# A two-layer transformer block in float32: one plain matmul for each weight product in place of three of split parts, a ring of wider weight units without loops, and a feed-forward in one pass

## What is computed

```python
def swiglu(h, w_in, w_out):
    g, u = jnp.split(h @ w_in, 2, axis=-1)
    return (jax.nn.silu(g) * u) @ w_out          # w_in 1024 x 5632, w_out 2816 x 1024

def adaln(cond, prm):                            # two rows of cond, mod_w 1024 x 9216
    mod = jax.nn.silu(cond) @ prm["mod_w"] + prm["mod_b"]
    return jnp.split(mod, N_MOD, axis=-1)

def half_ffn(x, m, name):
    sh, sc, g = m
    h = modulate(rms_norm(x, prm[name + "_norm"]), sh, sc)
    return x + 0.5 * g * swiglu(h, prm[name + "_w_in"], prm[name + "_w_out"])
```

## Time and profile before

| | us |
|---|---|
| median of 3 runs | 4154.09 (4153.86 to 4158.08) |
| span of the profiled execution | 4147.5 |
| PE busy | 3665.2 (88%), 21992 matmul records |
| DVE busy | 2043.7 (49%) |
| ACT busy | 1508.2 (36%) |
| POOL busy | 263.8 (6%) |
| DMA | 478.14 MB, 115 GB/s on average |

### The profile page before, as it was taken

How to read it: one execution, slowest core, us unless ns; L and a number is a source line. 1 busy time by engine, 2 the same in 40 slices (tenths; PEclk the granted TensorE clock), 3 DMA queues, 4 the chain that set the end, 5 groups by cost and what they waited for, 6 DMA issues and landing times. The chain is left out here.

```text
span 4147.5 us, 57916 instructions
## 1 busy us (share of the span) xinstructions
PE 3665.2 (88%) x21992; PEld 3092.6 (75%) x21992; DVE 2043.7 (49%) x2625; ACT 1508.2 (36%) x1826; POOL 263.8 (6%) x182
## 2 busy tenths in 40 slices
PE   6899987788999999988889898967999998769898
PEld 5688842366887678866579898846889898648898
DVE  6733347444334743331455555455455555554455
ACT  3522311233223532221244444334344544253343
POOL 0000010100001000020100102110000102200001
PEclk9999998899999999999899999978999999878999
DMA  8633330012334923342026565501646565204464
GB/s 263 206 84 104 87 77 32 21 31 82 96 88 144 300 78 100 83 105 81 1 79 180 148 182 153 158 1 36 165 136 178 161 179 170 77 0 107 135 172 133
DMA packets 807729, 478.14 MB, mean 115 GB/s; under 512 B 33413, under 2 KB 806004, under 8 KB 807428
## 3 DMA queue, kind: packets, MB, share of 16 engines
q1 hardware_dynamic: 797200, 473.13, 39.8%
q10 hardware_dynamic: 10356, 2.63, 0.4%
HBM read 474.65 MB, written 1.05 MB: 115 GB/s over the span
## 5 line engine op out<-in xcount | busy, mean ns | idle before, releaser
L469 PE MATMUL psum<-normed,weights_part 128*128 128x256 f32 (+1 forms) x11232 | 1732.9, 316 | 92.5 <-DVE normed L1025 32.6
L469 PEld LDWEIGHTS psum<-normed,weights_part 128*128 128x128 f32 x11232 | 1588.2, 192 | 231.6 <-issue 89.6
L453 DVE TENSOR_TENSOR weights_part<-weights,weights_part 128x2048 fp32r<-128x2048 f32 x460 | 1053.0, 2292 | 806.3 <-ACT weights_part L445 805.7
L445 ACT ACTIVATE weights_part<-weights 128x2048 fp32r<-128x2048 f32 x460 | 878.3, 1912 | 866.7 <-PE psum L469 360.0
L469 PE MATMUL psum<-hidden,weights_part 128*128 128x256 f32 (+1 forms) x4224 | 681.0, 323 | 10.6 <-DVE hidden L1037 10.6
L469 PEld LDWEIGHTS psum<-hidden,weights_part 128*128 128x128 f32 x4224 | 615.4, 190 | 74.3 <-DVE hidden L1037 12.7
L398 POOL TENSOR_TENSOR square<-square,rinvs 128x256 f32<-128x256 f32 (+1 forms) x52 | 82.5, 1586 | 2694.6 <-ACT rinvs L383 2691.7
L469 PE MATMUL psum<-weights_part,cond_part 128*2 128x256 f32 x1728 | 214.2, 280 | 13.8 <-DVE weights_part L453 13.8
L469 PEld LDWEIGHTS psum<-weights_part,cond_part 128*2 128x2 f32 x1728 | 138.8, 83 | 70.0 <-issue 14.5
L1035 DVE TENSOR_TENSOR rinvs<-rinvs,psum 128x256 f32<-128x256 f32 (+1 forms) x88 | 45.5, 517 | 174.1 <-ACT rinvs L947 174.1
L1047 DVE SCALAR_TENSOR_TENSOR x<-psum,gate,x 128x256 f32 (+1 forms) x112 | 49.7, 480 | 163.6 <-PE psum L469 163.5
(11 more groups left out here) (295 smaller groups left out, 3136.6 us busy)
## 6 DMA issues: line engine op xcount, KB each, us to landing
weights<-in_l_ffn_w_in SPq DMA_DIRECT2D x176, 512.0 KB, 5.0
weights<-in_ffn_w_gu SPq DMA_DIRECT2D x176, 512.0 KB, 5.0
weights<-in_l_mod_w SPq DMA_DIRECT2D x72, 1024.0 KB, 5.1
weights<-in_w_in SPq DMA_DIRECT2D x34, 1024.0 KB, 5.0
weights<-in_w_gate SPq DMA_DIRECT2D x64, 512.0 KB, 4.8
weights<-in_l_ffn_w_out SPq DMA_DIRECT2D x64, 384.0 KB, 4.1
weights<-in_ffn_w_down SPq DMA_DIRECT2D x64, 384.0 KB, 4.1
weights<-in_l_ffn_w_out SPq DMA_DIRECT2D x64, 320.0 KB, 3.4
```

Of the source, the lines that this page charges most:

```text
L445: nc.scalar.activation(k.parts[part][0][:, :], k.slots[slot][:, 0:WIDE], ACT.Copy).then_inc(high.sem, 1)
L453: nc.vector.tensor_tensor(k.parts[part][1][:, :], k.slots[slot][:, 0:WIDE], k.parts[part][0][:, :].bitcast(F32), ALU.subtract).then_inc(lo ...
L469: mm = k.nc.tensor.matmul(to, left[a], right[b], start=first and n == 0, stop=last and n == len(PASSES) - 1)
```

## The change

1. Every split product becomes one plain float32 matmul. `split_high`, `split_low`, `product_of_parts`, the part buffers and the splits of activations are gone.
2. The ring is one area of 15360 words in each partition, in which units of their own size follow each other; a unit may be loaded when the last unit that overlapped its place is done. A feed-forward up unit is now a pair of hidden chunks (2 MB, 4096 words), a down unit 256 output columns over 11 chunks (2816 words), a conditioning unit 512 columns (2 MB), a merge unit 256 columns of one branch. The loops of four are written out.
3. The feed-forward is one pass: 11 up units, then 8 down units, with all 22 hidden chunks in memory. A sum over 22 chunks stays in its bank.
4. DVE adds the squares, all but the last, which the matmul with ones now takes as a second matmul into the same bank. In the conditioning ACT copies the products out of PSUM.

```diff
-def product_of_parts(k, to, left, right, first, last):
-
-    for n, (a, b) in enumerate(PASSES):
-        mm = k.nc.tensor.matmul(to, left[a], right[b], start=first and n == 0, stop=last and n == len(PASSES) - 1)
-    return mm
...
+def place_units(k):
+    units = [u for spec in k.plan for u in spec.units]
+    head, raised = 0, [0] * LANDINGS
+    for j, u in enumerate(units):
+        if head + u.words > RING_WORDS:
+            head = 0
+        u.at = head
+        head += u.words
+        u.slot = k.ring[:, u.at:u.at + u.words]
+        shared = [i + 1 for i, v in enumerate(units[:j]) if v.at < u.at + u.words and u.at < v.at + v.words]
+        u.free_after = max([0, j - LANDINGS + 1] + shared[-1:])
...
+def load_weights(k, sp, done):
+    while k.loaded < len(k.units) and k.units[k.loaded].free_after <= done:
+        u = k.units[k.loaded]
+        if u.free_after:
+            sp.wait_ge(*k.units[u.free_after - 1].done)
+        for dst, src in u.load(u.slot):
+            sp.dma_start(dst, src).then_inc(k.weights_ready[u.landing], 16)
+        k.loaded += 1
...
+def sum_of_squares(k, bank, tokens):
+    total, buffers = square_buffers(k, tokens)
+    k.nc.tensor.matmul(bank, k.const("ones"), total, start=True, stop=False)
+    return k.nc.tensor.matmul(bank, k.const("ones"), buffers[(KD - 1) % 2], start=False, stop=True)
...
 def half_ffn(k, tokens, name, layer, gain, shift, gate):
...
         @block.tensor
         def _(pe):
-            nc.tensor.matmul(k.psum[:, 0, T], k.const("ones"), k.square[:, 0, T], start=True, stop=True)\
-                .then_inc(t["summed"].sem, 1)
...
+            sum_of_squares(k, k.psum[:, 0, T], tokens).then_inc(t["summed"].sem, 1)
+            for c in range(PAIRS):
+                W = wait_weights(k, pe, up, c).rearrange("p (t k c) -> p t k c", t=2, k=KD)
+                places = [(2 * c + half, side) for half in range(2) for side in range(2)]
+                order = [(n, side, kc) for n, side in places for kc in range(KD)]
+                if c == 0:
+                    pe.wait_ge(t["inverse_done"].sem, t["inverse_done"].base + 1)
+                    order = [(n, side, kc) for kc in range(KD) for n, side in places]
+                for n, side, kc in order:
+                    if (n, side) == (0, 0):
+                        pe.wait_ge(t["normed"].sem, t["normed"].base + kc + 1)
+                    if n >= 4 and (side, kc) == (0, 0):
+                        pe.wait_ge(t["gated"].sem, t["gated"].base + n - 3)
+                    at = (n % 2) * P
+                    mm = nc.tensor.matmul(k.psum[:, 2 * (n % 4) + side, T], W[:, side, kc, at:at + P], k.normed[:, kc, T],
+                                          start=kc == 0, stop=kc == KD - 1)
...
+            for c in range(8):
+                W = tiled(wait_weights(k, pe, down, c), KH, 256)
+                for u in range(2):
+                    chunk, half = (c // 2) * 2 + u, c % 2
+                    for kc in range(KH):
+                        n = half * KH + kc
+                        if chunk == 0:
+                            pe.wait_ge(t["gated"].sem, t["gated"].base + max(n + 1, KF - 2))
...
+                        mm = nc.tensor.matmul(k.psum[:, (chunk + 4) % 8, T], W[:, kc, u * P:(u + 1) * P], k.hidden[:, n, T],
+                                              start=n == 0, stop=n == KF - 1)
...
 def conditioning(k, l):
...
             def unit(i, c):
-                slot, weights = wait_parts(pe, i, c)
                 for kc in range(KD):
-                    mm = product_of_parts(k, k.psum[0:2, 2 * slot, 0:256], [x[:, kc, :] for x in cond_parts],
-                                          [wide_tile(w)[:, kc, :] for w in weights], kc == 0, kc == KD - 1)
+                    mm = nc.tensor.matmul(k.psum[0:2, c % 4, :], k.cond[:, kc, :], W[:, kc, :], start=kc == 0, stop=kc == KD - 1)
```

More of the change, by code:

```diff
@@ L481, in _ @@
         def _(act):
-            if splits is not None:
-                splits[0](act, 0, 0)
             act.wait_ge(mean.sem, mean.base + 1)
@@ L494, in _ @@
                                                bias=shift(c, cond), scale=gain(c, cond))
-            if parts is not None:
-                for c in range(KD):
-                    act.wait_ge(scaled.sem, scaled.base + 2 + c)
-                    k.nc.scalar.activation(parts[0][:, c, T], dst[:, c, T], ACT.Copy).then_inc(high.sem, 1)
         @block.tensor
         def _(pe):
-            k.nc.tensor.matmul(k.psum[:, 0, T], k.const("ones"), k.square[:, 0, T], start=True, stop=True)\
-                .then_inc(mean.sem, 1)
+            sum_of_squares(k, k.psum[:, 0, T], tokens).then_inc(mean.sem, 1)
         @block.vector
         def _(dve):
-            if splits is not None:
-                splits[1](dve, 0, 0)
             dve.wait_ge(root.sem, root.base + 1)
@@ L585, in add_product_of_parts @@
-    high.close(KD), low.close(KD)
+            for n in range(KD):
+                dve.wait_ge(formed.sem, formed.base + n + 1)
+                for cond, part in (halves(tokens) if gate is not None else [(0, T)]):
+                    row, product = k.x[:, n, part], k.psum[:, n, part]
+                    if gate is None:
+                        last = nc.vector.tensor_tensor(row, row, product, ALU.add)
+                    else:
+                        last = nc.vector.scalar_tensor_tensor(row, product, gate(n, cond), row, ALU.mult, ALU.add)
+                last.then_inc(added.sem, 1)
+                if n >= 2:
+                    add_square(k, dve, tokens, n - 1)
@@ new lines, in _ @@
+            if shift is not None:
+                for c in range(KD):
+                    act.wait_ge(t["scaled"].sem, t["scaled"].base + c + 1)
+                    for cond, part in parts_of_tokens:
+                        last = nc.scalar.activation(k.normed[:, c, part], k.rows[c % 2][:, part], ACT.Identity,
+                                                    bias=shift(c, cond), scale=gain(c, cond))
+                    last.then_inc(t["normed"].sem, 1)
+            for n in range(KF):
+                act.wait_ge(t["formed"].sem, t["formed"].base + 2 * n + 2)
+                if n >= 2:
+                    act.wait_ge(t["gated"].sem, t["gated"].base + n - 1)
+                nc.scalar.activation(k.rows[n % 2], k.psum[:, 2 * (n % 4), T], ACT.Silu).then_inc(t["silu_done"].sem, 1)
@@ L1056, in half_ffn @@
+        stream_ahead(k, block, down)
+    for name, n in dict(summed=1, root_done=1, inverse_done=1, scaled=KD if shift is not None else 0, normed=KD, formed=2 * KF,
+                        silu_done=KF, gated=KF, out_formed=16, out_added=KD).items():
         t[name].close(n)
@@ L2277, in program @@
         k.x = sb("x", [P, KD, TOK])
-        k.slots = [sb(f"weights{s}", [P, SLOT]) for s in range(RING)]
+        k.ring = sb("weights", [P, RING_WORDS])
         k.q_stage, k.r_stage = sb("q_stage", [P, 2, LAT]), sb("r_stage", [P, 2, LAT])
@@ L2306, in program @@
                         tokens = LAT
[L2307 to L2311 removed]
+                add_product(k, k.spec(f"out{l}"), tokens, k.mix, mix_gate(k))
             half_ffn(k, tokens, "ffn2", l, *modulated(k, 2), half_gate(k, 1))
```

761 lines of the change are left out of this document (265 added, 496 removed).

## The result

| | before | changed |
|---|---|---|
| median of 4 runs each, us | 4153.98 (4146.68 to 4158.08) | 4652.34 (4651.70 to 4659.56) |
| span of the profiled execution, us | 4147.5 | 4651.1 |
| PE busy, us | 3665.2 (88%) | 4277.5 (92%) |
| matmul records | 21992 | 15266 |
| DVE and ACT busy, us | 2043.7 and 1508.2 | 831.2 and 554.8 |

The changed kernel takes 1.121 times as long (95% interval 1.119 to 1.122): about 500 us more. The forecast was 4694 us with a range of 4635 to 4775. The median lies inside, 42 us under the forecast.

What follows compares the result with a forecast made beforehand. The prediction took PE, through what a product costs there, to bound the kernel. Its terms 294 + 281 + 42 - 77 = +540 on 4147.5 gave 4687, plus 6.6 to the median: 4694 us, range 4635 to 4775.

Steps and rivals of the forecast that it cites:

- Part 1: On PE, one plain product costs more than three split matmuls: +294 us with 512 tokens, +281 us with 256.
- the rival of two passes: Products on PE: a plain matmul has one record, not two, so products get cheaper; 3115 us, chance 0.03.
- The rival of four full passes: Products on PE: a plain matmul costs four times a split pass; +269 us, 4963 us, chance 0.03.
- Part 2: Conditionings: units of 512 columns take 7.95 us, 18 of them 143 us where 36 took 122, twice: +42 us.
- Part 3: Ring and weight loads: wider units and written-out loops cost nothing, as loads keep up with PE.
- Its cover: Conditioning loads: 264 GB/s needed against 289 GB/s measured, a margin of 9%.
- Part 4: Stage seams: PE's waits for splits, low parts and the last square come back, net -77 us, ends -130 and -20.
- first units: First unit of each feed-forward, paced by low parts: 10 us come back over eight.
- second ones matmuls: Norms: the added matmul with ones costs at most 2 us, 0.6 on average, 8 us for 13.
- before ones: Seams before the ones matmul: the last GpSimd square goes, 1.26 or 0.72 us each, about 10 us over twelve.
- The starts: Feed-forward starts: only a split and a low part fall out, 1.5 us each for eight; 6 us for two second-block norms.
- the rival of larger seams: Seams: all 143 us of idle time and the squares come back, no price for ones; 4610 us, chance 0.02.

Runs made afterwards that it cites:

- Experiment 1: Kernel before with each product as one plain float32 matmul of the high parts; splits, ring and loops stay, low parts unused: 4759.25 us, ratio 1.147.
- Experiment 4: Changed kernel with a ring of 8192 words for 15360, one 2 MB unit ahead instead of two: 4679.48 us, ratio 1.128.
- experiment 6: Changed kernel with one fp32r pass of a fixed tile for each conditioning product, weights loaded but not used: 4561.81 us, ratio 1.099.
- experiment 8: Changed kernel with one fp32r pass against a fixed tile for every product but the output projections, loads kept: 2606.36 us, ratio 0.628.
- experiment 5: Kernel before with the last square folded into a ones matmul and, in twelve stages, the first unit in plain matmuls on unsplit data: 4112.23 us, ratio 0.9909.
- experiment 3: Kernel before with the last square taken by a second matmul with ones instead of the GpSimd add: 4134.11 us, ratio 0.9962.
- experiment 2: Changed kernel with three fp32r passes against one fixed tile for each product, output projections still plain, nothing split, loads kept: 4083.42 us, ratio 0.984.
- experiment 7: Changed kernel with three fp32r passes per product, output projections plain, loads kept; in feed-forwards each pass takes a different fixed stationary tile: 4083.56 us, ratio 0.984.

## Why the prediction held, and where it was off

**Part 1, the product's price, is shown.** The eight feed-forwards came out nearly as it said: 455.7 us for 453, and 230.3 for 228. Experiment 1 puts the same price into the old structure and gets the same feed-forwards. The two records for one plain matmul, read from the counts of rows 5, decided the sign: the rival of two passes is out by 1500 us.

The rival of four full passes is out as well, by 311 us. The Trainium skill ("FP8 and Floating Point Precision", TensorE Precision Notes) has four passes for true FP32. The cost measured here bears that out, though no run shows the passes one by one; what failed in that rival was to price a pass at the distance of a split matmul. In a stream at clock 1.00, the higher of TensorE's two levels (2.4 GHz), four times 256 columns are 0.427 us, and 0.4326 are measured; once 256 columns are 0.107, and the split pass takes 0.120. So each split matmul carries some 13 ns over its columns, and a plain one 6 ns over all four passes. Four passes for three cost 20% with 256 columns (26% with 512), and not 33%.

**Part 2, the conditioning:** a unit takes 7.94 us for the 7.95 predicted. The term of +42 came out as +36, since the stage before was 125 and 126 us long and not 122; I had multiplied a steady unit by 36 and left out how the stage starts.

**Part 3, no cost of the ring, holds**: no group waits for weights. Its cover was named right and sized wrong. Experiment 4 shows that a ring of one unit ahead would have cost 27 us, at the starts of stages, and experiments 6 and 8 that the load rate was never near.

**Part 4 is the step that was mis-sized.** With the in-stage parts of its -77 taken apart (hidden waits 10.6 and first units 10 back, second ones matmuls 8 added), it says -64 between stages. Measured are -98:

| idle between stages, us | predicted | measured |
|---|---|---|
| starts of the eight feed-forwards | -12 | -24.2 |
| starts of the second block's two input projections | -6 | -11.4 |
| before ones | -10 | -19.7 |
| output projections | -16 | -19.3 |
| conditionings | -9 | -10.5 |
| merges | -10.7 | -8.7 |
| attentions and the rest | 0 | -4.5 |

The 10.7 us that the largest group of PE waited for weight parts stand in this table at the merges: two waits of 5.15 us there and one of 0.40 inside a feed-forward.

**The starts** are the largest miss, half of it: "only a split and a low part fall out", 1.5 us each, gave 3.0, and 5.7 at a projection for 3. Timeline of the start of a feed-forward with 256 tokens, before:

```profile
3034.49 1.19 PE L964 MATMUL psum<-square,consts 128*128 128x256 f32 x2 [3.26 <-PEq L534]
3034.52 1.91 ACT L445 ACTIVATE weights_part<-weights 128x2048 fp32r<-128x2048 f32 x1 [1.74 <-PEq L534]
3036.44 1.28 ACT L927 ACT_TABLE_LOAD   x1
3037.74 0.47 ACT L927 ACTIVATE roots<-psum,eps 128x256 f32<-128x256 f32 x1
```

and changed:

```profile
3425.83 1.28 ACT L812 ACT_TABLE_LOAD   x1 [0.27 <-PEq L457]
3425.87 0.67 PE L391 MATMUL psum<-square,consts 128*128 128x256 f32 x2 [1.22 <-PEq L457]
3427.13 0.47 ACT L812 ACTIVATE roots<-psum,eps 128x256 f32<-128x256 f32 x1
```

A split of 1.91 us stood on ACT ahead of the square root's table load, and with it the root came 3.25 us after the start of ones; now it comes after 1.26 us, in spite of the second ones matmul. My sum had counted the splits that PE waits for, and not those that stand in a queue ahead of the norm chain. That this is the cause is shown in the kernel of before: in experiment 5 the split of the first unit and the low part are gone from such a start, and the wait is that of the changed kernel, 3.0 us. With the last square folded alone (experiment 3) it is 6.2 to 6.4 in the second block.

**Before ones**, the add that I priced at 10 us gave 12 in experiment 3 (43.8 to 31.7 over all stages). Another 7.5 came at the ends of the output projections (5.7; the one with 512 tokens waits 5.5 us before, 4.0 in experiment 3, 1.9 changed) and of the first conditioning (4.9, 3.6, 1.7), of which my sum had nothing. Timelines at the end of that output projection, experiment 3:

```profile
933.89 1.66 DVE L588 SCALAR_TENSOR_TENSOR x<-psum,mod,x 128x256 f32<-128x256 f32 x4 [9.22 <-PE psum L475]
...
936.29 1.26 POOL L398 TENSOR_TENSOR square<-square 128x512 f32<-128x512 f32 x1 [8.15 <-ACT square L383]
```

and changed:

```profile
1049.64 0.88 DVE L485 SCALAR_TENSOR_TENSOR x<-psum,mod,x 128x256 f32<-128x256 f32 x2 [5.39 <-PE psum L471]
```

Before, two chunks of x are added together when a unit is done, and GpSimd adds the seventh square behind them; now each chunk is added as it is done, so one is left at the end, and DVE adds the square. No run undoes these two alone, so their shares stay open.

Inside stages the sum is good: lengths of +602.0 measured, +604 by my terms (294 + 281 + 42 + 8 - 10.6 - 10). With the products and the conditioning as they came out, the seams are worth some -107 us net (503.6 less 294, 281 and 36): between my -77 and the end of -130. So the measured time lies 42 us from the forecast and 42 us from the rival of larger seams, 4610 (4618 by the terms named there). What I held against that rival, the norm chain, does remain: 34 us of waits at the eight starts. But the chain itself got shorter.

Of the 10 us for first units about half came. Over the pure stream, a feed-forward of 256 tokens had 5.2 us too much before (195.3 for 190.1) and has 2.2 now, and 2.1 of that gain are the hidden waits. Stretches at the start of one, in the kernel before and in the changed one (columns as in experiment 2):

```profile
3041.90:3051.90 10.00, 9.91 (x62) 9.94 (x63) 9.68 (x16) 7.29 (x9) 0.00 (x0) 0.72 0.02 5
3051.90:3061.90 10.00, 10.00 (x86) 10.00 (x85) 6.06 (x7) 3.53 (x7) 0.00 (x0) 1.00 0.76 207
```

```profile
2445.00:2455.00 10.00, 10.00 (x34) 8.38 (x35) 2.38 (x6) 4.85 (x8) 0.00 (x0) 0.73 0.00 1
2455.00:2465.00 10.00, 10.00 (x48) 8.79 (x48) 0.84 (x2) 0.77 (x2) 0.00 (x0) 1.00 0.20 64
```

In both kernels the first ten microseconds behind the gap hold seven tenths of the records of the next ten, with PE busy nearly all the time: the granted clock stands at 0.72 and 0.73. So it was the clock that paced the first unit before, and it still does; the low parts cost little, by my estimate 0.5 us a start (what the excess lost, less what the clock accounts for). Over the five short feed-forwards of the changed kernel the first ten microseconds have clocks of 0.73, 0.71 and three times 0.83, and the excess over 228.1 is 2.8, 2.9 and three times 1.7 us, with no wait to see.

The last 5 us: I added 6.6 us from span to median. The changed kernel's profiled run took 4652.94 us, 1.8 above its span. The offset came from one run against a median of others and was mostly scatter.

## What to carry to other kernels

Before one kind of matmul is put in place of another, find how many records the profile writes for one instruction (divide the count of a line by the program's count), and take the price from the distance between starts in a stream. Work on DVE and ACT that runs beside a bound PE is nearly free: the changed kernel has 2165 us less of it, and everything but the product's price gave back some 107 us, nearly all at the seams. There, look not only for the splits that PE waits for, but for those that stand in a queue ahead of the norm chain or of a stage's last rows. The two best kernels here keep the split products and change only the seams (one add folded into a matmul, one first unit in plain float32). When a ring holds units of several sizes, work out where they come to lie: room for one unit ahead can be room for none. A load rate in a stage where nothing waits for DMA is a demand; to know the ceiling, make the compute cheap and look again.

## What the hardware showed that I had not expected

- One core's weight loads reached 368 GB/s in the conditioning and 348 in a feed-forward when PE no longer held them back, against a highest slice of 300 in the earlier trace rows.
- A plain float32 product costs four times its bare columns at the full clock and almost nothing more: 0.4326 us for 256 columns, where four times the columns are 0.427, and 0.858 for 512, where they are 0.853.
- The fp32r pass with 512 columns takes 0.2267 us in the kernel before and 0.2333 in steady stretches of the changed structure (experiments 2, 7 and 8, with three passes or one), at a clock of 1.00 in both, while with 256 columns and in plain float32 the two structures don't differ. The repeated stationary tile is excluded; whether it is the order of the banks, the place of the activations or the program without loops wasn't tried.
- The granted clock at the start of a feed-forward was 0.69 to 0.85 over the first ten microseconds in every kernel profiled. In the changed kernel that goes with 1.7 to 2.9 us over the pure stream, without a wait in the trace.
